# A value block between the last recurrent levels of a two-block diffusion transformer on one Trainium2 core

## The reference

```python
h_lat = modulate(rmsnorm(x_lat, norm_pre_mix[l]), sh1, sc1)      # the same for ctx
# h @ w_in gives, 512 columns each: q, k, v, hq, forget z (2 directions), i, gate g
s = einsum("bhiqd,bhikd->bhiqk", q, k) * DA_HEAD_DIM ** -0.5      # 4 heads, i = 0, 1
p = softmax(s); a = p[:, :, 0] - lam * p[:, :, 1]
out_da = rmsnorm(a @ v, da_subln) * (1.0 - lambda_init)
S_next = exp(b_end) * S + (k * exp(b_end - bcum)).T @ v           # recurrence over tokens
out_hg = rmsnorm(o_forward + o_backward, hg_norm) * silu(hg_g)
y_lat = concatenate([out_da, out_hg]) @ w_out
u_ctx = rms_norm(ctx_2, norm_g) * (1.0 + sc_c) + sh_c             # second block's context
```

## Time and profile before

| | |
|---|---|
| median of 3 runs | 1107.05 us (1105.41 to 1107.17) |
| the profiled execution | 1104.74 us, of which the span of the page is 1102.9 us |
| TensorE busy | 924.7 us (84%) |
| VectorE, ScalarE, GpSimd busy | 333.4, 208.2, 48.5 us |
| mean granted TensorE clock | 0.938 |
| read from HBM | 308.66 MB, 281 GB/s over the span |

### The profile page before, as it was taken

How to read it: one execution, slowest core, us unless ns; L and a number is a source line. 1 busy time by engine, 2 the same in 40 slices (tenths; PEclk the granted TensorE clock), 3 DMA queues, 4 the chain that set the end, 5 groups by cost and what they waited for, 6 DMA issues and landing times.

```text
span 1102.9 us, 11355 instructions
## 1 busy us (share of the span) xinstructions
PE 924.7 (84%) x4456; PEld 476.1 (43%) x4456; DVE 333.4 (30%) x597; ACT 208.2 (19%) x449; POOL 48.5 (4%) x113
## 2 busy tenths in 40 slices
PE   4999999989889879877676676666767989999997
PEld 2666564754544523222222222222223766654773
DVE  2299523491461431111111101101113265422022
ACT  2222321221462311000000000000004113411121
POOL 0200000000200100000000000000001000000000
PEclk9899999999999989988888888888889999999999
DMA  9964541642779769999999999999999288004200
GB/s 349 344 237 153 191 161 68 232 150 76 255 278 410 291 236 428 427 428 428 428 429 428 428 430 428 428 429 430 428 428 398 101 300 310 0 20 153 77 1 38
DMA packets 65623, 310.20 MB, mean 281 GB/s; under 512 B 2753, under 2 KB 4980, under 8 KB 52916
## 3 DMA queue, kind: packets, MB, share of 16 engines
q1 hardware_dynamic: 63124, 301.04, 68.2%
q0 software_dynamic: 2464, 8.68, 2.3%
HBM read 308.66 MB, written 1.05 MB: 281 GB/s over the span
## 4 chain that ended last, share of the span: by engine, by line
PE 59%; DMA 31%; DVE 4%; ACT 2%; issue 2%; SPq 1%; POOL 1%; POOLq 0%; DVEq 0%; ACTq 0%
PE bank L846 35%; DMA ring<-w_up_dram 25%; PE bank L1227 8%; DMA ring<-w_down_dram 4%; PE bank L1510 2%; PE bank L865 2%; DMA ring<-w_in_dram 2%; PE bank L1417 1%; PE bank L1247 1%; PE bank L993 1%; PE bank L876 1%; PE bank L1423 1%; PE bank L1260 1%; PE bank L1447 1%; PE bank L1192 1%
## 5 line engine op out<-in xcount | busy, mean ns | idle before, releaser
L1227 PE MATMUL bank<-ring,ilat 128*32 128x512 f32 x984 | 151.2, 767 | 102.2 <-DMA ring<-w_up_dram 101.1
L1227 PEld LDWEIGHTS bank<-ring,ilat 128*32 128x32 f32 x984 | 41.5, 135 | 207.9 <-issue 206.8
L2333 DVE TENSOR_TENSOR state<-state,bank 64x512 f32<-64x512 f32 x16 | 11.0, 690 | 304.5 <-ACT state L1760 304.5
L846 PE MATMUL bank<-ring,hT 128*128 128x512 f32 x224 | 96.9, 592 | 0.0
L846 PE MATMUL bank<-hT,ring 128*128 128x256 f32 (+1 forms) x320 | 88.0, 436 | 4.0 <-DVE hT L1954 2.0
L846 PE MATMUL bank<-ring,kT 128*128 128x512 f32 (+1 forms) x192 | 82.2, 584 | 3.4 <-ACT kT L1540 2.6
L846 PEld LDWEIGHTS bank<-hT,ring 128*128 128x128 f32 x320 | 62.5, 197 | 28.7 <-issue 21.5
L1247 PE MATMUL bank<-ring,ilat 128*32 128x512 f32 x512 | 58.9, 596 | 14.8 <-ACT ilat L1764 12.6
L846 PEld LDWEIGHTS bank<-ring,hT 128*128 128x128 f32 x224 | 42.4, 190 | 53.2 <-issue 52.1
L1260 PE MATMUL bank<-state,ilat 128*128 128x512 f32 x128 | 59.2, 605 | 0.9 <-DVE state L2337 0.9
L1760 ACT ACTIVATE state<-bank 64x512 f32<-64x512 f32 x16 | 9.4, 590 | 255.0 <-PE bank L1227 255.0
(11 more groups left out here) (353 smaller groups left out, 1045.5 us busy)
## 6 DMA issues: line engine op xcount, KB each, us to landing
ring<-w_down_dram SPq DMA_DIRECT2D x32, 2048.0 KB, 23.7
ring<-w_up_dram SPq DMA_DIRECT2D x31, 2048.0 KB, 23.3
ring<-w_gate_dram SPq DMA_DIRECT2D x30, 2048.0 KB, 18.8
ring<-w_ada_dram SPq DMA_DIRECT2D x24, 2048.0 KB, 9.2
ring<-w_in_dram SPq DMA_DIRECT2D x8, 2048.0 KB, 13.7
ring<-fno_w_in_dram SPq DMA_DIRECT2D x4, 2048.0 KB, 12.6
ring<-w_out_dram SPq DMA_DIRECT2D x2, 2048.0 KB, 9.3
ring<-mla_w_in_dram SPq DMA_DIRECT2D x2, 2048.0 KB, 18.2
```

The source lines that it names most:

```text
L846: ins = pe.matmul(o, l, r, start=start and i == 0, stop=stop and i == len(terms) - 1)
L1227: ins = pe.matmul(bank[0][32 * t:32 * t + 32, :], xin_cur[:, j, :], x[:, n0:n0 + TN], start=j == 0, stop=j == J - 1)
```

## The change

One of the value blocks is taken out of the row behind the rotary products and put between level 5 and level 6; the gate's two blocks go behind the other three value blocks. The weight tiles `("in", 2)` and `("in", 7)` change places in the stream. GpSimd's root for the recurrent rows goes ahead of the router's clearing and loads. VectorE writes the recurrent rows one block in item 0 and one in item 1, the first heads' rows in item 4 in place of 3, and scales the context rows ahead of the gate. The context pieces of the second block go from items 4 and 5 to 5 and 6, those with g = 1 from ScalarE to VectorE, and the transposes of recurrent rows from items 2 and 3 to 4 and 6.

```diff
-        for t in (None, 4, None, 6, None, 5, None, None, 1, None, None, 0, None, 7, 2):
+        for t in (None, 4, None, 6, None, 5, None, None, 1, None, None, 0, None, 2, 7):
             if t is None:
                 mod_tile(next(order))
             else:
...
         claim_levels(5)
+        pclaim(("v", 0))
         claim_levels(6)
         claim_levels(7)
         for s in range(2):
             for n in range(2):
                 pclaim(("rot", s, n))
+        for b in range(1, 2 * TB):
+            pclaim(("v", b))
         for b in range(TB):
             pclaim(("g", b))
-        pclaim(("v", 0))
-        pclaim(("v", 1))
-        pclaim(("v", 2))
-        pclaim(("v", 3))
         claim(("cross", 0), 4 + lb_turn[0] % 4)
         claim(("cross", 1), 4 + (lb_turn[0] + 1) % 4)
         lb_turn[0] += 2
...
 
-        context_work = [(), (), ((0, 0),), ((0, 1),), ((1, 0),), ((1, 1),), (), ()]
+        context_work = [(), (), ((0, 0),), ((0, 1),), (), ((1, 0),), ((1, 1),), ()]
+        mix_work = {4: 0, 6: 1}
 
         nq = 0
         for b in range(TB):
...
                         claim(("gt", GATE_MODS[n - 1]), 7)
-                if n in (2, 3):
-                    claim(("mixT", n - 2, 1), 4)
+                if n in mix_work:
+                    claim(("mixT", mix_work[n], 1), 4)
         claim(("mod", GATE_MODS[-1]), 7)
...
             root_inverse(0, TB, "rstd_c2")
-            wait_filled(pool, ("v", 2 * TB - 1))
+            wait_filled(pool, ("g", TB - 1))
...
             wait_filled(pool, ("oh", TB - 1))
             for i, n in enumerate(("norm_post_mix", "norm_post_ffn")):
                 pool.dma_start(post_norm[i][:, :], a[n][0].partition_broadcast(P)).then_inc(sem("post_in"), 16)
+            root_inverse(0, TB * HEADS, "rstd_oh")
             pool.memset(qh[:, 0:J * 32], 0.0).then_inc(sem("router_set"), 1)
             pool.wait_ge(sem("router_set"), 1)
             for h in range(2):
                 pool.dma_start(router4[:, h], a["w_router"][0].rearrange("(h p j) e -> h p j e", p=P, j=4)[h])\
                     .then_inc(sem("router_in"), 16)
-            root_inverse(0, TB * HEADS, "rstd_oh")
             pool.wait_ge(sem("eps_sums"), 1)
             root_inverse(0, HEADS, "rstd_o", eps=eps_sums)
             pool.wait_ge(sem("eps_sums"), 2)
...
             level(5)
+            wv = wait_tile(pe, ("in", 2))
+            tokens_out(("v", 0), wv, hT3, 0)
             level(6)
             level(7)
             for s, x in enumerate((q3, k3)):
...
                                         start=True, stop=True)
                     fills(ins, ("rot", s, n))
+            for b in range(1, 2 * TB):
+                tokens_out(("v", b), wv, hT3, b)
             w = wait_tile(pe, ("in", 7))
             for b in range(TB):
                 tokens_out(("g", b), w, hT3, b)
-            w = wait_tile(pe, ("in", 2))
-            for b in range(2 * TB):
-                tokens_out(("v", b), w, hT3, b)
...
+                if n in mix_work:
                     pe.wait_ge(sem("scratch_done"), 1)
-                    turn_chunks(("mixT", n - 2, 1), mix[:, n - 2, :], 1)
+                    turn_chunks(("mixT", mix_work[n], 1), mix[:, mix_work[n], :], 1)
                 if n:
...
             take_heads("q", 1)
-            decays(11, 12)
-            decays(12, 14)
+            def take_value(b):
+                o = wait_filled(act, ("v", b))
+                frees(st, act.activation(v3[:, b, :], o[:, :], ACT.Copy), ("v", b))
+
+            decays(11, 14)
+            take_value(0)
 
             st.did(act.activation(QF_.rearrange("p (h t) -> p h t", t=P), Bc[0][:, :, 1:P + 1], ACT.Exp))
             kb3 = Bc[1].rearrange("p (h b) t -> p h b t", b=TB)
...
-            for b in range(TB):
-                o = wait_filled(act, ("g", b))
-                st.did(act.activation(gb[:, b * TN:(b + 1) * TN], o[:, :], ACT.Tanh, scale=0.5), sem("gb_tanh"))
-            for b in range(2 * TB):
-                o = wait_filled(act, ("v", b))
-                frees(st, act.activation(v3[:, b, :], o[:, :], ACT.Copy), ("v", b))
-                if b == 1:
+            for b in range(1, 2 * TB):
+                take_value(b)
+                if b == 2:
                     act.wait_ge(sem("ctx2_in"), 16)
                     for i in range(TB):
                         square(c2[:, i, :], i, D, i == TB - 1)
+            for b in range(TB):
+                o = wait_filled(act, ("g", b))
+                st.did(act.activation(gb[:, b * TN:(b + 1) * TN], o[:, :], ACT.Tanh, scale=0.5), sem("gb_tanh"))
             for d in range(2):
                 o = wait_filled(act, ("cross", d))
                 frees(st, act.activation(XFB[:, d * TN:(d + 1) * TN], o[:, :], ACT.Copy), ("cross", d))
...
                         square(o[:, i * P:(i + 1) * P], 4 * b + i, P, i == HEADS - 1)
-                for bg in context_work[n]:
-                    take_context(*bg)
-                if n in (2, 3):
-                    take_mix(n - 2, 1)
+                for b_, g in context_work[n]:
+                    if g == 0:
+                        take_context(b_, g)
+                if n in mix_work:
+                    take_mix(mix_work[n], 1)
                 if n:
...
 
+            dve.wait_ge(sem("rstd_c2"), 1)
+            for b in range(TB):
+                step(dve.tensor_scalar(c2[:, b, :], c2[:, b, :], rr[:, b:b + 1], None, ALU.mult), "c2_normed")
+
             for b in range(TB):
...
-            dve.wait_ge(sem("rstd_c2"), 1)
-            for b in range(TB):
-                step(dve.tensor_scalar(c2[:, b, :], c2[:, b, :], rr[:, b:b + 1], None, ALU.mult), "c2_normed")
-
-            def recurrent_out():
+            def recurrent_out(b):
...
+                if b == TB - 1:
+                    st.settle()
+                    step(dve.memset(cf[:, 8:9], 0.0), "scratch_done")
+
+            def take_context(b, g):
+                o = wait_filled(dve, ("c2T", b, g))
+                for jj in range(4):
+                    j = 4 * g + jj
+                    ins = dve.tensor_scalar(uT[:, j, b * P:(b + 1) * P], o[:, jj * P:(jj + 1) * P],
+                                            mc[:, MLAC, 1, j:j + 1], mc[:, MLAC, 0, j:j + 1], ALU.mult, ALU.add)
+                    frees(st, ins, ("c2T", b, g)) if jj == 3 else step(ins)
+
+            def head_out(b):
+                dve.wait_ge(sem("rstd_o"), b + 1)
+                o = bank[turns[("o", b)][0]]
...
                     da_difference(n + 1)
                 if n + 2 < len(da):
                     da_max(n + 2)
-                if n == 0:
-                    recurrent_out()
+                if n < TB:
+                    recurrent_out(n)
+                if n == HEADS:
+                    head_out(0)
                 if n > 1 and GATE_MODS[n - 2] not in LATER_GATES:
                     gate_rows(n - 2)
-                if h == HEADS - 1:
-                    dve.wait_ge(sem("rstd_o"), b + 1)
-                    o = bank[turns[("o", b)][0]]
-                    for i in range(HEADS):
-                        ins = dve.scalar_tensor_tensor(mix[:, b, i * P:(i + 1) * P], o[:, i * P:(i + 1) * P],
-                                                       rr[:, 4 * b + i:4 * b + i + 1], subln[:, :], ALU.mult, ALU.mult)
-                        frees(st, ins, ("o", b)) if i == HEADS - 1 else step(ins)
-                    st.settle()
-                    step(dve.memset(cf[:, 8:9], 0.0), "mix_ready")
+                for b_, g in context_work[n]:
+                    if g:
+                        take_context(b_, g)
+            head_out(1)
```

More of the change, by code:

```diff
@@ L1646, in _ @@
             st.did(act.activation(QB_, QB_, ACT.Exp), sem("end_decay"))
+            for b in range(1, 2 * TB):
+                take_value(b)
+                if b == 2:
+                    act.wait_ge(sem("ctx2_in"), 16)
+                    for i in range(TB):
+                        square(c2[:, i, :], i, D, i == TB - 1)
             for b in range(TB):
@@ L1649, in _ @@
                 st.did(act.activation(gb[:, b * TN:(b + 1) * TN], o[:, :], ACT.Tanh, scale=0.5), sem("gb_tanh"))
-            for b in range(2 * TB):
-                o = wait_filled(act, ("v", b))
-                frees(st, act.activation(v3[:, b, :], o[:, :], ACT.Copy), ("v", b))
-                if b == 1:
-                    act.wait_ge(sem("ctx2_in"), 16)
-                    for i in range(TB):
-                        square(c2[:, i, :], i, D, i == TB - 1)
             for d in range(2):
@@ L2155, in _ @@
                                               .broadcast_to([P, HEADS, P]), ALU.mult, ALU.mult))
-            dve.wait_ge(sem("rstd_c2"), 1)
-            for b in range(TB):
-                step(dve.tensor_scalar(c2[:, b, :], c2[:, b, :], rr[:, b:b + 1], None, ALU.mult), "c2_normed")
-            def recurrent_out():
+            def recurrent_out(b):
                 dve.wait_ge(sem("rstd_oh"), 1)
```

(19 more changed lines are left out.)

## The result

| | before | changed |
|---|---|---|
| median | 1106.23 us, 4 runs (1104.31 to 1107.17) | 1095.73 us, 4 runs (1093.72 to 1096.86) |
| ratio, 95% interval | | 0.9907 (0.9887 to 0.9926) |
| profiled execution | 1104.74 us | 1093.72 us |
| span | 1102.9 us | 1091.9 us |

What follows compares the result with a forecast made beforehand. TensorE's chain to the output projection was taken as the bound, the expert loads moving with it. -5.74 + 0.5 - 3.8 = -9.0 us, replay -9.5, taken -9.3: 1107.05 - 9.3 = 1097.8 us, range 1095.3 to 1102.0 us.

Steps and rivals of the forecast that it cites:

- Part 1: Value block moved between levels 5 and 6 fills TensorE's idle time and avoids the slow clock behind it: -5.74 us.
- a gain of only 4.1 us where the clock doesn't fall: Levels 5 to 6: part of the 1.63 us might be missing in unprofiled runs, leaving between 4.1 and 5.7 us.
- Part 2: Output gate last before the scores: second pair's bank waits for tanh and VectorE's product, +0.5 us, bounds 0 and 1.3.
- The cover for the exponentials and the rotary bank: Behind the moved value block: later exponentials are free, rotary bank is free 0.2 us before TensorE wants it; failure costs tenths.
- Parts 3 and 4: Attention items: earlier root, split recurrent rows and moved pieces cut TensorE's waits, -3.8 us, bounds 0 and -5.9 us.
- The replay: Four engine queues replayed from the cross term with row durations, present and new order; gave -9.5 us for the whole change.
- (a): Attention items: waits removed in one item return in the next, only the moved value block counts; 1101.8 us, chance 0.13.
- (b): Output projection: weight loads become the bound; 3 us longer landings lose 2 us, 1099.8 us; chance 0.06.
- (c): Levels 5 to 6: value block waits for weights or level 6 misses its operands, gap stays; 1103.7 us, chance 0.05.
- (d): Attention items: TensorE's clock falls, making the kernel slower, 1116 us with 20 us of slow matmuls; chance 0.04.

Runs made afterwards that it cites:

- filler: Kernel before plus four unused products of 512 columns on TensorE in the idle time between levels 5 and 6; ratio to before 0.9993.
- items-only: Changed kernel with levels, gate, values and their weight tiles as before, keeping the edits of root, recurrent rows and pieces; ratio to before 0.9930.
- tuned: Gate ahead plus item 4's gate row before the first heads' rows and the last item's gate product before the product with v; 1092.53 us, ratio 0.9890.
- block alone: Kernel before with only the first value block moved between levels 5 and 6, its weight tile loaded first; 1098.44 us, ratio 0.9923.
- gate ahead: Changed kernel with the gate's two blocks again ahead of the last three value blocks and the context rows scaled behind them; ratio to before 0.9911.
- gap left: Changed kernel with the moved value block one place later, between levels 6 and 7, so the idle time before level 6 stays; ratio to before 0.9949.

## Why the prediction was right, and where it was not

**Part 1, -5.74 us: right in size, -5.88 us measured; its reason was wrong in one term.** Nearly all of the 0.14 us are a matter of ends: I let the block start 2.05 us after level 5, and it starts 225.85 - 223.96 = 1.89 us after. I split the gain into 4.08 us of idle time and 1.63 us of slow clock, as if each could be had alone. The filler removes the slow clock, and 1.63 us should come back; 0.02 us do, since VectorE's chain (operands of level 6, keys of level 7, rotary banks) bounds the same 14.8 us. What the block does is to put 6.88 us of useful work beside that chain: from level 5 to the next block it is 239.75 - 223.96 = 15.79 us with the block and 14.79 us without it, so the block costs 1.00 us in place of 6.88 us. The sum came out since it was made from TensorE's positions and not from the two terms. For the same reason a gain of only 4.1 us where the clock doesn't fall can't come about here: the filler kernel is the gap without the clock's fall, and its scores come at 56.07 us all the same. I had drawn that alternative from the Trainium skill (TensorE: Matmul & The Clock Gate, "What's actually happening"), which says that the clock is low after idleness and, of a kernel's start, that the number of slow matmuls changes from run to run; the first agrees with the stretches (0.53 behind 4.08 us of idle time), and the second no row shows for this place: in the three profiled kernels that have the gap, level 6 takes 3.41, 3.36 and 3.24 us from start to start.

**Part 2, +0.5 us: right,** 0.62 us with what follows in the items. The cover for the exponentials and the rotary bank held: no wait stands ahead of the 80 products at 239.75 us.

**Parts 3 and 4, -3.8 us: right in kind, a sixth too small.** The term alone is -4.52 us, as the items-only kernel has it; the -3.89 us of the changed kernel include part 2. The replay named the three remaining waits, 0.57, 0.43 and 1.16 us; they are 0.17, 0.41 and 1.09 us. Idle time from the rows undercounts what a wait costs from start to start; the replay counts it, and its -9.5 us was nearer to 9.77 us than the sum of -9.0 us. The middle of the two wasn't the better number. Part by part it is -5.88 + 0.62 - 4.52 = -9.78 us, where I had -9.0 us. Of the 2.1 us between the time and its forecast, 1.1 us are this difference in the gain and 0.9 us the start: I took 1107.05 us, the median of three executions, and 23 later ones have 1106.11 us.

**Rivals.** (a) falls by the items alone. (b) falls: the changed and the tuned kernel's projections run without a wait. (c) falls by the timeline. (d) falls: 287 to 331 us has the clock at 1.00 in the changed kernel's stretches. The case in the Trainium skill (same page, "A second HAM failure mode: psum-queue depth-cycling"), in which small idle times between groups of matmuls make the clock swing, isn't seen in the items.

**What the runs leave open.** The profiled span shrank by 11.0 us, the edited path by 9.77 us. The rest is 2.16 us lost ahead of level 5 and 3.28 us gained in routing and first expert: from the projection to the first reload 58.88 us, against 62.16 us. Neither belongs to the edit, as the last section shows. In the medians the block alone and the items alone gained 7.7 and 6.7 us, where their paths gained 5.88 and 4.41 us, and the two together are more than the changed kernel has. The clock is probably part of it: the median of the mean granted clocks is 0.942 in the six executions of the block alone and 0.936 in the 23 of before, and taking away the slow 3.5 us (0.53 to 1.00) gives only 0.0015 of that. Why those executions met the better clock isn't settled.

## What to carry to other kernels

Idle time of the busiest engine behind another engine's chain is worth as much as the work that fits beside that chain (here 6.88 us of work for 1.00 us of delay). So look for a block whose operands have long been ready, move it there, and cost it by the positions of the busiest engine, not by adding up idle time and slow clock. Before counting a stall as gain, ask what stands second in the same stretch; four products in the idle time told it. And put small operations on a side engine (a root ahead of loads, a row ahead of another) in the order in which the main engine waits for them: with the moved pieces that gave 3.9 of the 9.8 us here. Check what each move puts in the way of another: the moved heads' rows brought a new wait of 1.09 us, which the tuned kernel removes.

## What was not expected of the hardware

TensorE's clock differs between profiled kernels in stretches that no edit touches, and between executions of one kernel. Routing and first expert took 58.88, 59.74, 61.65, 62.16 and 63.05 us from projection to first reload in the changed kernel, gate ahead, tuned, before and gap left, and the filler kernel, whose path is that of before, had 58.87 us. TensorE's rows of before and of the tuned kernel show the first expert's products at 8.77 us, those of the changed kernel at 7.07 us; first the tuned kernel:

```profile
384.33 8.77 PE L1230 MATMUL bank<-ring,ilat 128*32 128x512 f32 x64 [0.98 <-DVE ilat L2342]
```

```profile
388.25 7.07 PE L1228 MATMUL bank<-ring,ilat 128*32 128x512 f32 x64 [0.97 <-DVE ilat L2338]
```

That is 1.70 of the 3.28 us between before and changed; a product just ahead (L1192 in before, L1193 in changed) has the rest, 3.50 against 1.91 us. The same 28 us of routing have a granted clock of 0.76 before, 0.88 in the changed and the filler kernel and 0.70 in the gap-left kernel.

The 2.16 us ahead of level 5 are of the same kind. The stretch from 27 to 58 us, before and changed (columns as in the earlier trace rows):

```profile
27.00:58.00 31.00, 28.96 (x151) 20.00 (x150) 9.40 (x26) 6.72 (x15) 6.63 (x12) 0.90 1.03 349
```

```profile
27.00:58.00 31.00, 28.97 (x145) 20.78 (x144) 7.19 (x24) 6.61 (x15) 6.69 (x12) 0.80 1.03 349
```

Changed, items only and gap left have 0.80 or 0.81 there and start level 5 at 223.51 to 223.97 us; the other seven have 0.89 or 0.90 and start it at 221.80 to 222.84 us. Gate ahead and tuned are among the seven, with all edits of the items, so it isn't the edit of the items, and the block alone, which loads the two tiles in the new order, starts level 5 at 221.94 us.

Between executions of before, the mean granted clock runs from 0.933 to 0.944: of the 23, the twelve at 0.936 or less have a median of 1107.7 us and the eight at 0.939 or more 1105.1 us. With a spread of 4 us in one stretch, a change of 3 us in the path can be told by the positions in one profile and hardly by ten executions.
